# Two unused bf16 products per step in the first attention and in both memory attentions

## The chip, the cores and the metric

The kernel runs on one core of one Trainium2 chip. Its metric is the device time of one execution in microseconds (us); a time quoted for a kernel is the median of several runs. A core has five engines that run side by side: TensorE (PE, matrix products into PSUM banks; its weight loads are listed apart as PEld), VectorE (DVE), ScalarE (ACT), GpSimd (POOL) and SyncE (SP, which issues the weight transfers here). The profile also lists the clock granted to TensorE, as a share of full speed: 1.00 is 2.4 GHz and 0.50 is 1.2 GHz.

## The reference, cut to what matters

The program is a chain of blocks on 512 tokens of width 1024. The first block is a mixer with two banded attentions, a gated convolutional feed-forward, a state-space layer and a second feed-forward; the second block is a convolution layer, a memory attention, a gated feed-forward, a differential attention, a second memory attention and a last feed-forward. The change touches the place where two functions are computed:

```python
def band_attention(q, k, v, n_prev, bias, sinks):      # called twice in the first layer
    ...
        sc = jnp.einsum("bqkgd,bskd->bkgqs", qb, kb).astype(jnp.float32) * scale + bias
    ...
            p = jax.nn.softmax(sc, axis=-1)
    ...
        return jnp.einsum("bkgqs,bskd->bqkgd", p.astype(vb.dtype), vb)

def memory_cross_attention(h, mem, w_q, w_k, w_v, w_o):  # called twice in the second block
    ...
    s = jnp.einsum('bshd,bmhd->bhsm', q, k, preferred_element_type=jnp.float32) * MEM_HEAD_DIM ** -0.5
    p = jax.nn.softmax(s, axis=-1)
    o = jnp.einsum('bhsm,bmhd->bshd', p.astype(v.dtype), v).reshape(B, S, D_MODEL)
    return o @ w_o
```

The first layer has 8 heads of width 64 whose band covers the whole causal past, with a learned relative bias, and 8 heads of width 64 with a short window, a linear bias and a sink per head. The memory attention has 4 heads of width 256 over 256 memory tokens.

## The kernel before, in words

Each engine has its own instruction stream, written out by hand, and the streams meet at semaphores. There is no scheduler and no planner: the order on an engine is the order of the Python code.

The large matrix products are in `gemm` (L546): a weight slab arrives by DMA, ACT rounds it to an upper half (`w_hi`, L1791), POOL subtracts to get the lower half (`w_lo`, L504), and PE runs three products per 128x128 weight block (L564, L565, L566), 512 columns each, into one of four banks.

The attentions of the first layer and of the memory are all in `attention` (L592). A *unit* is one head and one tile of 128 queries, and one *step* m of the loop at L647 handles four units at once, each at another stage:

- `score(m)` (L613) computes the scores of unit m. In the first layer these are fp32 products of 64 rows (`qk`) of 128 to 512 columns. For units 0 to 31 an fp32 product of 128 rows adds the learned bias (`rel,flip`) over all columns, and a bf16 product adds the mask (`masks_b,ident_b`, 128 columns). For units 32 to 63 one bf16 product adds the linear bias (`alibi_b,ident_b`). In the memory they are two fp32 products of 128 rows and 256 columns. The score of unit m waits until ACT has taken the exponential of unit m-3.
- DVE takes the row maximum (L1156) and the scale (L1158 or L1163), ACT the exponential (L1837), DVE the reciprocal and the division (L1172, L1175).
- `turn(m-3)` (L626) transposes the probabilities of unit m-3 on PE; ACT copies them out of the bank (L1849).
- `outputs(m-4)` (L640) multiplies them with the values. In the first layer the output of one product has 64 rows.

After 8 units (first layer) or 4 units (memory) the outputs of a group are complete, and ACT and DVE read them out (L1856, L1187). The first `outputs` of a later group waits until DVE is done with that (L635).

The first attention has 64 units and so 64 + 4 = 68 steps, each memory attention 16 units and 16 + 4 = 20 steps. The differential attention has a loop of its own and does not use this function, so `peers` is 1 in every call that is made.

`keep_clock(n)` (L576) issues n bf16 products of a 128x128 identity with 384 columns of the mask table, into columns 128 to 511 of bank 7, whose content nobody reads there. It is called with 8 ahead of the first attention (L685) and with 6 ahead of each memory attention (L708). Inside the step it stands behind `if peers == 2`, which no call fulfils.

Of the kernel before, what the change touches and what calls it, by code (L numbers as in the profile page):

```python
# [155 lines left out]
def build(nc, A, out, stages=ALL):  # L156
# [4 lines left out]
    with ExitStack() as ctx:  # L161
# [176 lines left out]
        def score_bank(n, peers):  # L338

            return bank[n % 3] if peers == 1 else bank[(0, 1, 2, 4)[n % 4]]  # L340

        def turned_bank(k, peers):

            return bank[3 + k % 2 if peers == 1 else 3]
# [196 lines left out]
        def _(pe):  # L541
# [34 lines left out]
            def keep_clock(n):  # L576


                for _ in range(n):
                    pe.matmul(NORM_BANK[:, P:4 * P], ident_b[:], masks_b[:], start=True, stop=True,  # L580
                              skip_group_check=True)
# [10 lines left out]
            def attention(units, groups, peers=1, out=None):  # L592


                U = len(units)
                u0, t0, g0 = au[0], at[0], ag[0]
                group_of = {first: g for g, (first, _, _) in enumerate(groups)}
                nch = len(groups[0][2])
                ends = {last: g for g, (_, last, _) in enumerate(groups)}

                def score(m):
                    tiles = range(peers * m, peers * (m + 1))

                    if tiles[-1] >= 2 + peers:
                        pe.wait_ge(a_exp, u0 + tiles[-1] - 1 - peers)
                    for k in range(len(units[tiles[0]].scores)):
                        for n in tiles:
                            u = units[n]
                            if u.rel is not None and n % NT == 0 and k == 1:
                                pe.wait_ge(rel_buf[u.rel % 4], 16 * (u.rel // 4 + 1))  # L610
                            l, r, c0, w = u.scores[k]
                            last = k == len(u.scores) - 1
                            mm = pe.matmul(score_bank(n, peers)[:, c0:c0 + w], l, r, start=(k == 0), stop=last,  # L613
                                           skip_group_check=True)
                            if last:
                                mm.then_inc(a_score, 1)

                def turn(m):
                    u = units[peers * (m + 1) - 1]
                    src = a_prob_t[:, peers * m % PROBS, :]  # L620
                    pe.wait_ge(a_prob, t0 + m + 1)

                    if m >= 3 - peers:
                        pe.wait_ge(a_pt, t0 + m - 2 + peers)
                    for kt in range(u.nk // P):
                        mm = pe.transpose(turned_bank(m, peers)[:, kt * P:(kt + 1) * P], src[:, kt * P:(kt + 1) * P],  # L626
                                          ident[:])
                    mm.then_inc(a_turn, 1)

                def outputs(m):  # L630
                    u = units[peers * (m + 1) - 1]
                    if peers * m in group_of:

                        held = group_of[peers * m] * nch + nch - 2
                        if held > 0:  # L635
                            pe.wait_ge(a_ol, g0 + held) if out is None else pe.wait_ge(o_raw, held)
                    pe.wait_ge(a_pt, t0 + m + 1)
                    nk = u.nk // P
                    for v, kt, ch, lo, hi, t in u.pv:
                        mm = pe.matmul(bank[5 + ch % 2][lo:hi, t * P:(t + 1) * P], v,  # L640
                                       a_pt_t[:, m % 2, kt * P:(kt + 1) * P], start=(kt == 0),
                                       stop=(kt == nk - 1), skip_group_check=True)
                    mm.then_inc(a_pv, 1)

                T = U // peers
                turn_lag, out_lag = (3, 4) if peers == 1 else (1, 2)
                for m in range(T + out_lag + (0 if out is None else 2)):  # L647
                    if m < T:
                        score(m)
                    if peers == 2:  # L650
                        keep_clock(2)
                    if out is not None and peers * m - 6 in ends:
                        out(ends[peers * m - 6])
                    if peers == 2 and 0 <= m - out_lag < T:
                        outputs(m - out_lag)
                    if 0 <= m - turn_lag < T:
                        turn(m - turn_lag)
                    if peers == 1 and 0 <= m - out_lag < T:
                        outputs(m - out_lag)
                au[0] += U  # L660
                at[0] += U // peers
                ag[0] += len(groups) * nch

            def attn():
                st = ST["attn_in"]

                def fin(c, j):
                    if isinstance(c, int) and c >= 13:
                        v_turn(v_tmp[:, c % 2, :], c - 13, BANKS + st.chunk0 + c + 1, S, bank[5 + c % 2])
                        return  # L670
                    pe.wait_ge(q_sq, c + 1)

                    if not isinstance(c, int) or c >= 2:
                        pe.wait_ge(q_root, c - 1)

                    pe.matmul(bank[5 + j % 2][:], head_ones[:], sq[:, j % 2, :], start=True, stop=True)\
                        .then_inc(q_sum, 1)

                def after(c, j):
                    first_sum(c, j)  # L680
                    if isinstance(c, int) and c == 0:
                        pe.wait_ge(cst_ready, 4)
                    lagged(fin, 17)(c, j)
                gemm(st, xh, xl, S, x_ready(KD * nrm[0]), after, peel=4, tail=6)
                keep_clock(8)  # L685
                pe.wait_ge(q_ready, 13)
                pe.wait_ge(flip_done, 2)
                pe.wait_ge(v_ready, 2 + 5)
                vt[0] = 5
                attention(*UNITS["attn"])  # L690
                gemm(ST["attn_out"], oh, ol, S, lambda k: pe.wait_ge(a_ol, k + 1))
# [14 lines left out]
            def mem(l):  # L706
                gemm(ST[f"mem_q{l}"], xh, xl, S, x_ready(KD * nrm[0]), first_sum, peel=4)
                keep_clock(6)  # L708
                pe.wait_ge(bank_free, BANKS + ST[f"mem_q{l}"].chunk0 + KD)
                pe.wait_ge(v_ready, 2 + vt[0])  # L710
                g0 = ag[0]
                attention(*UNITS["mem"])
                gemm(ST[f"mem_out{l}"], oh, ol, S, lambda k: pe.wait_ge(a_ol, g0 + k + 1))
# [1687 lines left out]
```

## Time and profile before

| | |
|---|---|
| median of 3 runs | 3370.28 us |
| the three runs | 3376.12, 3351.67, 3370.28 us |
| time of the profiled execution | 3372.42 us |
| its span, first to last instruction | 3370.6 us |
| mean granted TensorE clock | 0.960 |
| PE busy | 3145.2 us, 93% of the span |
| DVE, ACT, POOL busy | 47%, 38%, 38% |
| first attention, first score to first product of its output projection | 154.37 to 319.84 us |
| first memory attention, the same | 2045.72 to 2092.44 us |
| second memory attention, the same | 2894.32 to 2937.86 us |

The span is the time from the first to the last instruction on the core; the time of the execution is 1.8 us more. A busy share is the time in which the engine had an instruction under way. On PE, ends are modelled, so a PE that is always busy need not be at its peak: at half the clock the same work shows as more busy time. What a stage is bound by is read from what the engines wait for in that stage, and from the granted clock beside it.

### The profile page before, as it was taken

To read this page: it belongs to the slowest core of one execution; us is meant where nothing else is said; L and a number is where in the kernel's file an instruction comes from. 1 tells how busy PE (TensorE), PEld (TensorE's weight loads), DVE (VectorE), ACT (ScalarE), POOL (GpSimd) and SP (SyncE) were. 2 spreads that over 40 slices of the span, in tenths; PEclk is the share of its full clock that TensorE was granted. 3 is DMA by queue.
4 is the path that set the end of the run, shared out by engine and by line. 5 is a ranking of instruction groups with operands and counts; after the bars stand their busy time and mean duration, and the time that the engine had idled before them with its cause. 6 is when DMAs were issued, how large, how long until landed. Compare 5 with 4: busy or idle time off the path is not lost.

```text
span 3370.6 us, 40942 instructions
## 1 busy us (share of the span) xinstructions
PE 3145.2 (93%) x13890; PEld 2426.7 (72%) x13890; DVE 1576.5 (47%) x2266; ACT 1270.1 (38%) x1983; POOL 1274.5 (38%) x495
## 2 busy tenths in 40 slices
PE   7999999998998899999866698999999999899998
PEld 5655888886675578888743587888876787788886
DVE  6445555337616725551445843333237765332322
ACT  3244444333334534442312343434333343344432
POOL 3300444442341044444554641444442244144443
PEclk9996999999998899999988899999999999999999
DMA  3200222332220022223200221222331123122232
GB/s 133 78 16 13 94 93 93 97 102 75 79 84 1 1 94 94 93 94 100 94 31 25 75 94 43 90 94 93 99 101 55 63 94 94 44 94 93 93 100 88
DMA packets 73288, 260.48 MB, mean 77 GB/s; under 512 B 8528, under 2 KB 8792, under 8 KB 72928
## 3 DMA queue, kind: packets, MB, share of 16 engines
q1 hardware_dynamic: 68400, 249.07, 23.1%
q10 hardware_dynamic: 4784, 10.05, 0.8%
q8 instruction: 62, 1.02, 0.1%
q14 instruction: 42, 0.34, 0.0%
HBM read 256.97 MB, written 2.12 MB: 77 GB/s over the span
## 4 chain that ended last, share of the span: by engine, by line
PE 51%; issue 30%; POOL 13%; DVE 4%; ACT 2%; DMA 0%; ACTq 0%; POOLq 0%; DVEq 0%; SPq 0%
PE bank L564 12%; PE bank L566 12%; PE bank L565 12%; POOL w_lo L504 12%; PE bank L733 2%; PE bank L734 2%; PE bank L735 2%; PE bank L640 1%; PE bank L795 1%; POOL m_lo L517 1%; PE bank L1021 1%; PE bank L613 1%; PE bank L819 1%; PE bank L1024 1%; PE bank L909 0%
## 5 line engine op out<-in xcount | busy, mean ns | idle before, releaser
L504 POOL TENSOR_TENSOR w_lo<-w_raw,w_hi 128x1024 fp32r<-128x1024 f32 x475 | 1219.1, 2569 | 1948.8 <-ACT w_hi L1791 1948.7
L564 PE MATMUL bank<-xh,w_hi 128*128 128x512 f32 x2136 | 865.6, 405 | 94.8 <-POOL w_lo L504 63.2
L565 PE MATMUL bank<-xl,w_hi 128*128 128x512 f32 x2136 | 854.4, 400 | 0.0
L566 PE MATMUL bank<-xh,w_lo 128*128 128x512 f32 x2136 | 853.6, 400 | 0.0
L1791 ACT ACTIVATE w_hi<-w_raw 128x1024 fp32r<-128x1024 f32 x475 | 500.8, 1055 | 713.3 <-DMA w_raw<-w_glu_out 157.6
L564 PEld LDWEIGHTS bank<-xh,w_hi 128*128 128x128 f32 x2136 | 407.1, 191 | 212.3 <-POOL w_lo L504 71.1
L565 PEld LDWEIGHTS bank<-xl,w_hi 128*128 128x128 f32 x2136 | 407.1, 191 | 100.9 <-issue 4.1
L566 PEld LDWEIGHTS bank<-xh,w_lo 128*128 128x128 f32 x2136 | 407.1, 191 | 99.8
L1126 DVE TENSOR_TENSOR xt<-bank,xt 128x512 f32 x72 | 49.8, 692 | 501.5 <-PE bank L566 501.5
L566 PE MATMUL bank<-hh,w_lo 128*128 128x512 f32 x704 | 279.1, 396 | 0.0
L564 PE MATMUL bank<-hh,w_hi 128*128 128x512 f32 x704 | 279.1, 396 | 0.0
L565 PE MATMUL bank<-hl,w_hi 128*128 128x512 f32 x704 | 279.1, 396 | 0.0
L1707 DVE TENSOR_TENSOR f_u<-bank,rstd 128x512 f32<-128x512 f32 x88 | 60.8, 691 | 276.7 <-PE bank L566 276.7
L565 PEld LDWEIGHTS bank<-hl,w_hi 128*128 128x128 f32 x704 | 132.6, 188 | 32.3
L564 PEld LDWEIGHTS bank<-hh,w_hi 128*128 128x128 f32 x704 | 132.6, 188 | 32.3
L566 PEld LDWEIGHTS bank<-hh,w_lo 128*128 128x128 f32 x704 | 132.6, 188 | 32.3
L1710 DVE TENSOR_TENSOR f_h<-f_y,f_u 128x512 f32<-128x512 f32 x88 | 150.6, 1712 | 7.2 <-ACT f_y L2211 0.3
L2216 ACT ACTIVATE hh<-f_h 128x512 f32 x88 | 55.6, 632 | 260.6 <-DVE f_h L1710 260.6
L1100 DVE TENSOR_TENSOR acc<-acc,sq 128x512 f32<-128x512 f32 x88 | 103.1, 1172 | 70.2 <-ACT sq L1782 70.2
L564 PE MATMUL bank<-oh,w_hi 128*128 128x512 f32 x320 | 128.8, 403 | 0.2 <-issue 0.2
L566 PE MATMUL bank<-oh,w_lo 128*128 128x512 f32 x320 | 127.8, 399 | 0.0
L565 PE MATMUL bank<-ol,w_hi 128*128 128x512 f32 x320 | 127.7, 399 | 0.0
(302 smaller groups left out, 4278.8 us busy)
## 6 DMA issues: line engine op xcount, KB each, us to landing
w_raw<-w_ffn_in SPq DMA_DIRECT2D x88, 512.0 KB, 3.5
w_raw<-w_glu_in SPq DMA_DIRECT2D x88, 512.0 KB, 3.4
w_raw<-w_ffn_out SPq DMA_DIRECT2D x48, 512.0 KB, 3.5
w_raw<-w_glu_out SPq DMA_DIRECT2D x48, 512.0 KB, 3.5
w_raw<-w_ssm_in SPq DMA_DIRECT2D x41, 512.0 KB, 3.5
w_raw<-w_mem_kv SPq DMA_DIRECT2D x32, 512.0 KB, 3.5
w_raw<-w_pw SPq DMA_DIRECT2D x24, 512.0 KB, 3.4
w_raw<-w_diff_in SPq DMA_DIRECT2D x24, 512.0 KB, 3.5
```

The source lines that it names most:

```text
L504: pool.tensor_tensor(w_lo[:, slot, :], w_raw[:, slot, :], w_hi[:, slot, :].bitcast(F32), ALU.subtract).then_inc(w_split, 1)
L564: pe.matmul(b, wh, hi[:, k, 0:n], start=(k == 0), stop=False)
L565: pe.matmul(b, wh, lo[:, k, 0:n], start=False, stop=False)
L566: mm = pe.matmul(b, wl, hi[:, k, 0:n], start=False, stop=last)
L733: pe.matmul(b, wh, hi[:, k, 0:n], start=(k == 0), stop=False)
L734: pe.matmul(b, wh, lo[:, k, 0:n], start=False, stop=False)
L735: mm = pe.matmul(b, wl, hi[:, k, 0:n], start=False, stop=(k == KD - 1))
L1100: dve.tensor_tensor(acc[:], acc[:], sq[:, j % 2, :], ALU.add).then_inc(x_acc, 1)
L1707: dve.tensor_tensor(f_u[:], bu[:], rstd[:], ALU.mult).then_inc(bank_free, 1)
L1710: dve.tensor_tensor(f_h[:], f_y[:], f_u[:], ALU.mult).then_inc(f_prod, 1)
L1791: act.activation(w_hi[:, slot, :], w_raw[:, slot, :], ACT.Copy).then_inc(w_half, 1)
L2216: act.activation(row(hh, p), f_h[:], ACT.Copy)\
```

## The change

The condition in the step loop is dropped, so that two of the unused products are issued in every step of the first attention and of both memory attentions, between the scores and the transposes. Nothing else differs; a line is gone, so that lines after 650 have a number that is lower by one in the changed kernel.

```diff
@@ -647,8 +647,7 @@
                 for m in range(T + out_lag + (0 if out is None else 2)):
                     if m < T:
                         score(m)
-                    if peers == 2:
-                        keep_clock(2)
+                    keep_clock(2)
                     if out is not None and peers * m - 6 in ends:
                         out(ends[peers * m - 6])
                     if peers == 2 and 0 <= m - out_lag < T:
```

The order of the instructions shows where they stand. On PE, in the second half of the first attention (units with the linear bias; L613 scores, L626 transpose, L640 outputs, L580 the unused products):

```order
 L613 MATMUL bank<-alibi_b,ident_b 128x128
+L580 MATMUL bank<-masks_b,ident_b 128x384 x2
 L626 MATMUL bank<-ident,a_prob_t 128x128 x2
 L640 MATMUL bank<-a_pt_t,v_tok 64x128
 L613 MATMUL bank<-qk 128x256
 L613 MATMUL bank<-alibi_b,ident_b 128x256
+L580 MATMUL bank<-masks_b,ident_b 128x384 x2
 L626 MATMUL bank<-ident,a_prob_t 128x128 x2
 L640 MATMUL bank<-a_pt_t,v_tok 64x128 x2
```

Each step has one pair, behind its last score product and ahead of its transposes; there are 68 of these pairs in the first attention.

On PE, at the start of a memory attention (the scores of units 0 to 3, the first transpose, then unit 4):

```order
-L613 MATMUL bank<-m_k,m_q 128x256 x8
+L613 MATMUL bank<-m_k,m_q 128x256 x2
+L580 MATMUL bank<-masks_b,ident_b 128x384 x2
+L613 MATMUL bank<-m_k,m_q 128x256 x2
+L580 MATMUL bank<-masks_b,ident_b 128x384 x2
+L613 MATMUL bank<-m_k,m_q 128x256 x2
+L580 MATMUL bank<-masks_b,ident_b 128x384 x2
+L613 MATMUL bank<-m_k,m_q 128x256 x2
+L580 MATMUL bank<-masks_b,ident_b 128x384 x2
 L626 MATMUL bank<-ident,a_prob_t 128x128 x2
```

The eight score products that stood in a row have a pair behind every two of them; each memory attention gets 20 pairs. In all there are 108 pairs, 216 products. The streams of DVE, ACT, POOL and SP are the same as before.

## Rows read from the trace of the kernel before

**Rows 1.** The page, part 1 (busy time, share of the span, instructions).

```profile
PE 3145.2 (93%) x13890; PEld 2426.7 (72%) x13890; DVE 1576.5 (47%) x2266; ACT 1270.1 (38%) x1983; POOL 1274.5 (38%) x495
```

**Rows 2.** Stretches: length, busy time per engine, granted clock, DMA share, GB/s.

```profile
158.00:178.00 20.00, 20.00 (x46) 9.16 (x44) 6.25 (x25) 4.32 (x15) 0.00 (x0) 0.50 0.13 44
179.00:240.00 61.00, 61.00 (x304) 35.29 (x302) 28.25 (x99) 24.48 (x76) 0.00 (x0) 1.00 0.05 17
241.00:270.00 29.00, 25.40 (x145) 15.29 (x144) 21.83 (x95) 16.27 (x63) 0.00 (x0) 1.00 0.00 1
271.00:320.00 49.00, 48.98 (x157) 27.34 (x156) 24.24 (x107) 18.60 (x74) 0.00 (x0) 0.50 0.00 1
323.00:340.00 17.00, 17.00 (x74) 13.70 (x73) 5.33 (x8) 5.66 (x8) 5.78 (x3) 1.00 0.25 75
```

**Rows 3.** Timeline of PE, scores of units 32 and 48, and a group's first outputs.

```profile
242.26 0.49 PE L613 MATMUL bank<-qk 64*128 64x128 f32 x2
...
269.25 0.65 PE L640 MATMUL bank<-a_pt_t,v_tok 128*64 128x128 f32 x4 [1.13 <-ACT a_pt_t L1849]
...
271.85 0.58 PE L613 MATMUL bank<-qk 64*128 64x128 f32 x1
```

**Rows 4.** The same, tail of the first attention and its output projection's start.

```profile
314.32 0.69 PE L626 MATMUL bank<-ident,a_prob_t 128*128 128x128 f32 x2
...
319.84 0.80 PE L564 MATMUL bank<-oh,w_hi 128*128 128x512 f32 x1
320.43 0.63 PE L565 MATMUL bank<-ol,w_hi 128*128 128x512 f32 x1
...
321.71 0.48 PE L565 MATMUL bank<-ol,w_hi 128*128 128x512 f32 x1
```

**Rows 5.** Who waited for whom, 154 to 320 us: total us, times, longest.

```profile
DVE a_stat L1156 <- PE bank L613: 69.4, 53, 5.4
...
PE bank L640 <- ACT a_pt_t L1849: 3.2, 4, 1.3
```

**Rows 6.** Who waited for whom, first memory attention, 2040 to 2092 us.

```profile
DVE a_stat L1156 <- PE bank L613: 17.8, 13, 3.8
...
PE bank L640 <- DVE ol L1187: 8.7, 3, 3.2
```

**Rows 7.** Timeline from 154 us, and line L580 alone (ns: min/median/max).

```profile
153.75 0.65 PE L580 MATMUL bank<-masks_b,ident_b 128*128 128x384 bf16 x3
...
L580 PE MATMUL bank<-masks_b,ident_b x20: 326/326/336, 152.9 to 2894.1; 128*128 128x384 bf16 x20
```

**Rows 8.** Timeline of PE ahead of the first attention (start, us, instruction, count).

```profile
152.94 1.46 PE L580 MATMUL bank<-masks_b,ident_b 128*128 128x384 bf16 x8
154.37 0.46 PE L613 MATMUL bank<-qk 64*128 64x128 f32 x2
157.18 0.49 PE L613 MATMUL bank<-rel,flip 128*128 128x128 f32 x2 [2.35 <-DMA rel<-rel_table]
```

**Rows 9.** DVE's row maximum (L1156), one per unit, in 154:181 and in 181:241 us.

```profile
L1156 DVE TENSOR_REDUCE a_stat<-bank x7: 291/425/693, 157.8 to 177.3; 128x1 f32<-128x128 f32 x2, 128x1 f32<-128x256 f32 x2, 128x1 f32<-128x384 f32 x2, 128x1 f32<-128x512 f32 x1
...
L1156 DVE TENSOR_REDUCE a_stat<-bank x24: 291/490/692, 181.4 to 237.8; 128x1 f32<-128x512 f32 x6, 128x1 f32<-128x128 f32 x6, 128x1 f32<-128x256 f32 x6, 128x1 f32<-128x384 f32 x6
```

**Rows 10.** Stretches of the two memory attentions, columns as in rows 2.

```profile
2062.70:2066.10 3.40, 3.40 (x12) 2.94 (x13) 0.00 (x0) 0.00 (x0) 0.00 (x0) 0.50 0.00 0
...
2912.80:2916.00 3.20, 3.20 (x14) 2.86 (x13) 1.00 (x4) 0.84 (x3) 0.00 (x0) 0.50 0.02 5
```

**Rows 11.** Timeline of PE: both memory attentions' first scores and first projection product.

```profile
2045.72 3.72 PE L613 MATMUL bank<-m_k,m_q 128*128 128x256 f32 x16
...
2092.44 0.48 PE L564 MATMUL bank<-oh,w_hi 128*128 128x512 f32 x1
...
2894.32 3.72 PE L613 MATMUL bank<-m_k,m_q 128*128 128x256 f32 x16
...
2937.86 0.48 PE L564 MATMUL bank<-oh,w_hi 128*128 128x512 f32 x1
```

## The prediction, made before the changed kernel ran

> **What bounds the kernel now.** I read the busy shares first: PE is busy for 93% of the span [rows 1], so anything added to PE has to be looked at for its cover. The 40 slices show that its granted clock is below full in a few places, one of them the first attention. So the second view is a table of stretches through it [rows 2]. The reader is to see two low stretches: from 158 to 178 us and from 271 to 320 us the clock is 0.50 (1.2 GHz), between and after them 1.00 (2.4 GHz). In the long one PE is busy for 48.98 of 49.00 us, and with 157 matmul records in 49 us it gets through less than with 145 in 29 us at full clock. Being busy does not bring the clock back there. What PE did before it fell at 271 us: it had stood idle for 1.13 us at the start of a group of outputs, and before that its steps were half-filled products of 64 rows or 64 columns [rows 3]. What it did when the clock rose again: the output projection had begun, 128x128x512 products without a gap [rows 4]; the clock was back two microseconds later, and stayed [rows 2].
>
> The third view is who waits for whom. In the first attention DVE's row maximum waits for PE's scores 53 times, 69.4 us in all, while PE waits four times for ACT's copy, 3.2 us in all [rows 5]. So PE sets the pace there at either clock, and a product that is added to it is paid for unless it falls into one of those four gaps. The memory attentions are alike: DVE waits 17.8 us for scores, and PE stands idle three times, 8.7 us in all, until DVE has read out a group of outputs [rows 6].
>
> **The price of a pair.** Three of the same products end 0.65 us after the first has started and the last one takes 0.326 us, so they start 0.162 us apart at full clock, and a pair costs 0.324 us [rows 7]. The upper bound is the eight in a row ahead of the attention: 1.43 us from the first to the next score, 0.179 each with both edges, 0.36 a pair [rows 8]. At half the clock I take 0.65 (the projection's products start 0.43 us apart at 0.50, three of them from 320.43 to 321.71 us [rows 4], and 0.23 apart at 1.00, 74 in 17 us [rows 2], so nearly twice). There are 68 + 20 + 20 = 108 pairs, 35 us at full clock without any cover. The Trainium skill (TensorE: Matmul & The Clock Gate, Back-to-back issue gap) says that in a stream of weight loads and matmuls even 512 columns take about 131 ns each; by that a pair of 384 columns would be at most 0.26 us and the 108 pairs at most 28 us, 7 us less. The row of 0.162 us disagrees with it for this very product, and the sum goes by the row.
>
> **The sum, against the profiled execution's 3372.4 us** (2.1 us above the median of the three).
>
> 1. Units 0 to 31, the ones with the learned bias: 32 pairs at 0.324, PE without a gap [rows 2] and 24 units in 60 us [rows 9]: +10.4 us.
> 2. The low stretch of 20 us at their start. It begins after PE stood idle for 2.35 us until the first bias table had landed [rows 8]; the pair of step 0 comes behind that wait and cannot prevent it. How soon the clock returns with denser steps no row shows. One end: the clock returns after the same seven steps, whose pairs then cost 0.65, +2.3 us. The other: it returns at once, and half of 20 us is saved, -10. I take -4, that it returns some 8 us earlier, since the projection brought it back in two microseconds and the added products are as full as those, but they are only a fifth of a low step (seven steps in 20 us [rows 9]).
> 3. Units 32 to 47, at full clock now, 29.6 us from the score of unit 32 to that of unit 48 [rows 3]: 16 pairs are 5.2 us, of which the four gaps [rows 5] take in one each, 1.3 us: +3.9 us, so 33.5 us.
> 4. Units 48 to 63, the same work at half clock, take 42.5 us (271.85 to 314.32) [rows 3, 4]. If the pairs keep the clock, they take the same 33.5 us: -9.0 us.
> 5. The four last steps, without scores, and the first products of the projection: 5.5 us at half clock (314.32 to 319.84) become 2.8 and four pairs, 1.3: -1.4. Four product starts at 0.43 instead of 0.23 us apart: -0.8. Together -2.2 us.
> 6. Memory attentions: 20 pairs each. In steps 4, 8, 12 and 16 the outputs wait anyway (for ACT's first copy and for the three groups), and the pair ahead of them lies in that wait, since what ends it (DVE's reading, behind ACT's exponential of a unit whose score stands ahead of the pair) does not depend on the pair. The other 16 cost 5.2 us each time: +10.4 us for both.
> 7. Behind three of these waits in the first memory attention, and behind one in the second, the clock falls for 3.4 us [rows 10]. The first takes 46.7 us, the second 43.5 [rows 11], so that a low stretch costs 1.6 us. A pair shortens the idle time ahead from 3.2 to 2.8 us; one end is that all four go, -6.4, the other that one more comes, +1.6. I take one less: -1.6 us.
>
> The sum is 10.4 - 4.0 + 3.9 - 9.0 - 2.2 + 10.4 - 1.6 = +7.9 us: **3380 us**. Nothing is added on another engine or queue, the bank's columns are read by nobody at that time, and the products signal no semaphore, so the only thing queued behind a pair is PE's own next transposes and, through them, the next score; DVE's row maximum will wait for PE longer and ACT's copies come later by as much. What pays is the two attentions' steps, what is gained is the clock.
>
> **Rivals.**
>
> A. *The clock is not kept.* Where PE is busy already, the pairs add nothing to its busy time, and it sits at 0.50 while it is busy for 48.98 of 49.00 us [rows 2]. The Trainium skill (TensorE: Matmul & The Clock Gate, The HAM clock gate) says that the gate goes by how busy the engine has recently been; by that rule pairs in a gapless stretch would change nothing about the clock, and only their price would be left. Against it: with the same busy share the units with the learned bias, which have full 128-row products, run at 1.00 for 61 us [rows 2], so what fills the busy time matters, and the pairs are of the full kind. The time: units 48 to 63 stay at 42.5 and pay 16 x 0.65, 52.9 us instead of 33.5, +19.4; the tail 5.5 + 2.6 instead of 4.1, and 0.8 for the projection, +4.8; the first stretch at its upper end, +6.3; the memory +1.6. With +7.9 that is +40 us, **3412 us**, slower. It decides at the group boundary near 270 us: if PE's clock falls there although a pair has gone into the gap, this rival holds. Chance 0.13.
>
> B. *Both cures work.* The first low stretch goes at once (-6.0 beyond step 2's value) and all four in the memory too (-4.8): -3 us, **3370 us**, no change. For it: the projection needed only two microseconds. Against it: the idle times of 2.35 and 2.8 us stay. Chance 0.20.
>
> C. *The clock falls late or for a part* in units 32 to 63, half of A's 19.4 us: **3390 us**. Chance 0.12.
>
> D. *The pairs are hidden*, since DVE's and ACT's chain takes over at once; then only steps 2, 4, 5 and 7 are left, with the pairs of step 4 free as well: -4.0 - 12.9 - 3.5 - 1.6 = -22, **3350 us**. The 69.4 us that DVE waits for PE [rows 5] speak against it. Chance 0.05.
>
> That the low stretch from 271 us is an accident of the profiled run is possible: the fastest of the three runs is 20.7 us below it, and without that stretch it would be 12.9 + 3.5 = 16 us shorter. This makes no difference to the changed kernel's time, only to what it is compared with.
>
> **The numbers.** The forecast has 0.47, A 0.13, B 0.20, C 0.12, D 0.05, and 0.03 are for what I don't see. The predicted time is that of the likeliest case. Its own bounds: steps 2 and 7 at their good ends give 3370, and the median may differ from a profiled run by some 10 us, as the three runs do; at their bad ends, with 0.36 us a pair (+3.9), 3394, and with case C's half 3403. The range of 3360 to 3403 leaves out A and most of D, 0.18. About 1% (34 us) is what a measurement of this kernel can tell from no change. Faster by over 1% would be below 3337, which no case reaches: 0.02. Slower by over 1% is above 3404: A and a part of the rest, 0.14. Within 1%: 0.84.
>
> **What the profile would show.** L580 grows from 20 to 236 products of 0.326 us at full clock. Step 1: units 8 to 31 at a pace of 2.8 instead of 2.5 us a unit, clock 1.00. Step 2: the first low stretch ends before 178 us. Steps 3 to 5: clock 1.00 from there into the projection, 33 to 34 us for each 16 units with the linear bias, and the attention as a whole, 165.5 us before, within 3 us of that. Steps 6 and 7: about 52 and 49 us for the two memory attentions, 1.6 less for each low stretch that goes, idle times of 2.8 us at three group boundaries. The prediction is wrong if the clock is 0.50 anywhere in units 32 to 63, if a pair costs clearly more than 0.36 us in a step, or if the first attention changes by more than 15 us either way.

## The result, and the profile after

The changed kernel took **3379.9 us** (median of 11 runs, 3377.5 to 3389.4), beside 3361.3 us for the kernel before (11 runs, 3349.9 to 3376.1). The ratio is 1.0053, with a 95% interval of 1.0033 to 1.0073: half a per cent slower, within the 1% of "no change". The number forecast, 3380, was met; what it is compared with was not 3370, since two of the three runs known then are among the four longest of those eleven. Its scatter of 26 us against the 12 of the changed kernel is part of the story. One run of all those below (3559.6 us, of `e7_one`, at a mean granted clock of 0.829) was a slow one, and the ratios are taken without it.

The profiled execution of the change took 3383.0 us, its span 3381.2. First the page's busy times, then the stretches that answer to [rows 2] (length, busy us and instructions per engine, granted clock, DMA share, GB/s):

```profile
PE 3156.5 (93%) x14106; PEld 2439.1 (72%) x14106; DVE 1579.9 (47%) x2266; ACT 1269.9 (38%) x1983; POOL 1273.7 (38%) x495
```

```profile
158.00:168.00 10.00, 10.00 (x21) 3.73 (x20) 2.52 (x10) 1.69 (x6) 0.00 (x0) 0.50 0.08 33
...
172.00:240.00 68.00, 68.00 (x353) 40.39 (x351) 28.05 (x102) 23.96 (x76) 0.00 (x0) 1.00 0.07 20
...
245.00:316.00 71.00, 68.59 (x391) 41.28 (x389) 47.16 (x206) 36.36 (x141) 0.00 (x0) 1.00 0.00 1
...
316.00:340.00 24.00, 24.00 (x104) 19.31 (x103) 8.26 (x12) 8.66 (x12) 9.26 (x4) 1.00 0.21 68
```

The long low stretch is gone: 1.00 from 172 us into the projection. The low stretch at the start is still there, 13.7 us long instead of 20.5. The timeline of PE through the first attention (start, us, instruction, count, idle time before it) answers to [rows 3, 4, 8]:

```profile
157.63 0.80 PE L613 MATMUL bank<-rel,flip 128*128 128x128 f32 x2 [3.35 <-DMA rel<-rel_table]
...
249.61 0.48 PE L613 MATMUL bank<-qk 64*128 64x128 f32 x2
...
263.31 0.65 PE L640 MATMUL bank<-a_pt_t,v_tok 128*64 128x128 f32 x4 [0.54 <-ACT a_pt_t L1848]
...
269.19 0.70 PE L613 MATMUL bank<-qk 64*128 64x256 f32 x2
269.82 0.28 PE L613 MATMUL bank<-alibi_b,ident_b 128*128 128x256 bf16 x1
269.94 0.49 PE L580 MATMUL bank<-masks_b,ident_b 128*128 128x384 bf16 x2
...
271.16 0.70 PE L613 MATMUL bank<-qk 64*128 64x256 f32 x2
...
278.46 0.65 PE L640 MATMUL bank<-a_pt_t,v_tok 128*64 128x128 f32 x4 [0.54 <-ACT a_pt_t L1848]
...
280.90 0.48 PE L613 MATMUL bank<-qk 64*128 64x128 f32 x2
...
311.21 0.50 PE L580 MATMUL bank<-masks_b,ident_b 128*128 128x384 bf16 x2
...
316.00 0.51 PE L564 MATMUL bank<-oh,w_hi 128*128 128x512 f32 x1
```

Unit 32 begins at 249.61, unit 48 at 280.90, the first step without a score at 311.21, the projection at 316.00. A full step in between takes 1.97 us (269.19 to 271.16), with the pair behind its bias product. The idle time at a group boundary is 0.54 us where it was 1.13. Its place is ahead of the third outputs of a group (unit 42 here, as at 269.25 us in [rows 3], which calls them the first). What these outputs wait for is DVE's readout of the group before and what follows from it: the row maximum of unit 45, its exponential, and ACT's copy for unit 42:

```profile
275.89 0.69 DVE L1186 TENSOR_TENSOR ol<-bank,oh 128x512 fp32r<-128x512 f32 x1 [0.81 <-ACT oh L1855]
276.50 0.41 DVE L1155 TENSOR_REDUCE a_stat<-bank 128x1 f32<-128x256 f32 x1
...
277.59 0.45 ACT L1836 ACTIVATE a_prob_t<-bank,a_stat 128x256 f32<-128x256 f32 x1
...
278.04 0.37 ACT L1848 ACTIVATE a_pt_t<-bank 128x256 f32<-128x256 f32 x1
```

The memory attentions, as [rows 11] (first scores, outputs that wait for a readout, first product of the projection):

```profile
2042.96 1.13 PE L613 MATMUL bank<-m_k,m_q 128*128 128x256 f32 x4
...
2061.66 2.08 PE L640 MATMUL bank<-a_pt_t,m_v 128*128 128x128 f32 x8 [2.84 <-DVE ol L1186]
...
2094.59 0.48 PE L564 MATMUL bank<-oh,w_hi 128*128 128x512 f32 x1
...
2896.91 1.13 PE L613 MATMUL bank<-m_k,m_q 128*128 128x256 f32 x4
...
2915.60 2.08 PE L640 MATMUL bank<-a_pt_t,m_v 128*128 128x128 f32 x8 [2.84 <-DVE ol L1186]
...
2930.86 1.16 PE L640 MATMUL bank<-a_pt_t,m_v 128*128 128x128 f32 x8 [2.84 <-DVE ol L1186]
...
2943.43 1.16 PE L640 MATMUL bank<-a_pt_t,m_v 128*128 128x128 f32 x8 [2.29 <-DVE ol L1186]
...
2948.43 0.47 PE L564 MATMUL bank<-oh,w_hi 128*128 128x512 f32 x1
```

They take 51.6 and 51.5 us, where they took 46.7 and 43.5. The outputs at 2061.66 need 2.08 us for eight products (1.16 at full clock): the clock is low behind the wait. In the second memory attention it is low behind the first wait and again from 2932 us, behind the second, but not behind the third:

```profile
2915.00:2921.00 6.00, 5.40 (x20) 4.59 (x21) 1.55 (x5) 0.84 (x3) 0.00 (x0) 0.50 0.00 0
2932.00:2935.00 3.00, 3.00 (x12) 2.20 (x11) 1.00 (x4) 0.65 (x3) 0.00 (x0) 0.50 0.02 5
2936.00:2948.00 12.00, 9.71 (x74) 8.55 (x74) 3.81 (x12) 3.81 (x11) 0.00 (x0) 1.00 0.00 1
```

From rows like these, one table for all profiled runs. "Low" is the time at clock 0.50 in the first attention; the memory columns have the number of low stretches behind them, each of 3.4 us but for one of 6.8 us in the change. "Between" is from the first attention's projection to the first memory attention.

| profiled run | units 0-31 | 32-63 and tail | first attention | low | between | memory 1 | memory 2 |
|---|---|---|---|---|---|---|---|
| before | 87.9 | 77.6 | 165.5 | 72 | 1725.9 | 46.7 (3) | 43.5 (1) |
| after | 95.8 | 66.4 | 162.2 | 14 | 1727.0 | 51.6 (3) | 51.5 (2, one of 6.8 us) |
| e1_attn_only | 95.8 | 66.4 | 162.3 | 14 | 1727.0 | 43.6 (1) | 45.0 (2) |
| e2_mem_only | 89.3 | 70.5 | 159.8 | 51 | 1721.7 | 51.6 (3) | 51.3 (3) |
| e3_late | 89.2 | 66.4 | 155.6 | 24 | 1724.1 | 46.7 (3) | 43.5 (1) |
| e4_gaps | 79.5 | 62.0 | 141.5 | 0 | 1724.7 | 42.0 (0) | 41.9 (0) |
| e5_before_again | 85.1 | 85.0 | 170.2 | 85 | 1721.8 | 43.6 (1) | 45.1 (2) |
| e6_rows | 86.3 | 72.2 | 158.5 | 14 | 1725.8 | 46.7 (3) | 43.5 (1) |
| e7_one | 85.8 | 63.3 | 149.1 | 14 | 1725.3 | 45.1 (2) | 43.5 (1) |
| e9_start_mem | 85.7 | 85.6 | 171.3 | 89 | 1725.7 | 42.0 (0) | 41.9 (0) |
| e10, e13 | 85.7, 86.2 | 63.6, 63.6 | 149.3, 149.8 | 14, 14 | 1722.9 twice | 43.6 (1) twice | 45.2, 45.1 (2) |
| e11_gaps_longer | 80.3 | 62.0 | 142.2 | 0 | 1723.9 | 42.1 (0) | 42.1 (0) |
| e12_mem_filled | 90.0 | 77.6 | 167.6 | 75 | 1724.1 | 46.9 (0) | 46.9 (0) |

### The profile page after: what moved, and what is told of

Read it like the earlier page. It is cut to its first block, busy times and chain, and to the rows that moved or that the text cites. A ratio compares the mean times of both kernels' runs of the same rounds, so it can differ in the third digit from the quotient of the medians.

```text
span 3381.2 us, 41374 instructions
## 1 busy us (share of the span) xinstructions
PE 3156.5 (93%) x14106; PEld 2439.1 (72%) x14106; DVE 1579.9 (47%) x2266; ACT 1269.9 (38%) x1983; POOL 1273.7 (38%) x495
## 4 chain that ended last, share of the span: by engine, by line
issue 49%; PE 27%; POOL 20%; DVE 3%; ACT 1%; POOLq 0%; ACTq 0%; DMA 0%; DVEq 0%; SPq 0%
POOL w_lo L504 19%; PE bank L564 7%; PE bank L565 7%; PE bank L566 7%; PE bank L1020 1%; PE bank L640 1%; PE bank L613 0%; PE bank L908 0%; PE bank L1023 0%; PE bank L675 0%; PE bank L1037 0%; PE bank L982 0%; DVE s_dk L1520 0%; PE bank L962 0%; DVE s_ea L1513 0%
```

## The experiments

The kernels differ from the kernel before by the lines shown; nch is 1 in the first attention and 2 in the memory.

**e1_attn_only**

```diff
-                    if peers == 2:
+                    if nch == 1:
                         keep_clock(2)
```

> Pairs in the 68 steps of the first attention only, none in the memory attentions. Theory T1 (the profiled run of before had a low-clock stretch of 50 us in the units with the linear bias that its typical run, 11 us shorter, has only in part; the two memory attentions of the change pay 5 us each whatever the run): the first attention as in the changed kernel, 162 us, clock 1.00 from 171 us on; time 3380 less 10 to 13 us, so 3367 to 3370, and its runs lie within some 10 us. Rival T2 (the first attention gains 3 us against every run of before, and the memory attentions or what comes behind them cost the other 22): 3358 us.

Measured: 3367.3 us (3363.7 to 3371.5), ratio to before 1.0002 (0.9986 to 1.0018), clock 1.00 from 171 us. T1's number, and T2's 3358 us is out. The 12.6 us to the changed kernel come with the memory pairs, as their own price and as low stretches; by the table 51.6 + 51.5 less 43.6 + 45.0, 14.5 us.

**e2_mem_only**

```diff
-                    if peers == 2:
+                    if nch == 2:
                         keep_clock(2)
```

> Pairs in the 20 steps of each memory attention only. T1: 5 us for each, 1.6 us more or less for each 3.4 us low stretch that comes or goes: 3361 + 10 = 3371 us, with the wide scatter of before (25 us), since the low stretch of the first attention is there in some runs. T2: 3361 + 22 = 3383 us.

Measured: 3383.5 us (3364.5 to 3393.4), ratio 1.0047 (1.0021 to 1.0074), that is 16 us more than before (21 by the medians) in place of T1's 10. T2's number came out, but not its reason: in the profile the first attention has a low stretch of its own again, beginning at 285 us, and the stretch between the attentions is 4 us *shorter* than before. T1 was mis-sized: there are six low stretches in the memory and not four, which makes 3 us more; the rest of the difference has no row, and the eight runs lie 29 us apart.

**e3_late**

```diff
-                    if peers == 2:
+                    if nch == 1 and m >= 32:
                         keep_clock(2)
```

> Pairs only in steps 32 to 67 of the first attention (the units with the linear bias and the tail); none in units 0 to 31, none in the memory. T1: the 32 pairs of units 0 to 31 are pure price (10.4 us) except that they end the first low stretch some 6 us earlier, worth 3; the late ones keep the clock at 1.00 from unit 32 into the projection. 3368 - 10 + 3 = 3361 at the least good, and as low as 3354 if the low stretch at the start is as in before; its scatter is small. T2: no different from e1 but for the 10 us: 3348 us.

Measured: 3356.5 us (3353.5 to 3362.2), ratio 0.9977 (0.9958 to 0.9996), faster than before by little, within T1's 3354 to 3361, and with a scatter of 9 us. Units 32 to 63 take the same 66.4 us as in the change; units 0 to 31 take 6.6 us less, although the start's low stretch is 24 us here and 14 in e1. Its length turned out to be chance: with bare units 0 to 31 it is 14 us in e5, e6, e7, e10 and e13, and 20 to 24 in before, e2, e3 and e12. With 14 us in both (e1 and e10), and without the wait for the first bias table (3.3 and 3.7 us), the 32 pairs cost 92.5 - 82.0 = 10.5 us. T2 gave 8 us too little.

**e4_gaps**: no pairs; 120 products stand where PE waits. In the linear-bias units they are ahead of the outputs of units 34, 42, 50 and 58, so at four places and not at the five steps that the expectation names.

```diff
+                            if u.rel is not None and n == 0 and k == 1:
+                                keep_clock(12)
                             if u.rel is not None and n % NT == 0 and k == 1:
                                 pe.wait_ge(rel_buf[u.rel % 4], 16 * (u.rel // 4 + 1))
...
                         if held > 0:
+                            if nch == 2:
+                                keep_clock(14)
                             pe.wait_ge(a_ol, g0 + held) if out is None else pe.wait_ge(o_raw, held)
+                    if nch == 1 and m >= 34 and m % 8 == 2:
+                        keep_clock(6)
                     pe.wait_ge(a_pt, t0 + m + 1)
```

> No pairs in the steps; the unused products stand only where TensorE would idle: 12 ahead of the first wait for the bias table (idle 2.4 to 3.4 us), 6 in steps 34, 42, 50, 58 and 66 ahead of the outputs that wait 1.1 to 1.3 us for ACT, 14 ahead of each of the three waits for a group's readout in each memory attention (idle 2.3 to 3.2 us). If the clock falls because of these idle times and not because of what the steps are filled with: clock 1.00 throughout the three attentions, nothing paid, 3350 (fastest run of before) less up to 10 for the first stretch and 6 for the memory: 3336 to 3345 us. If it falls because the steps of the linear-bias units are too thin, the long low stretch still comes in some runs, and the scatter stays: 3350 to 3360 us.

Measured: **3342.3 us** (3340.1 to 3352.5), ratio 0.9935 (0.9911 to 0.9958). PE's timeline ahead of the first bias table, at two group boundaries of the linear-bias units, and at a readout wait of the memory; then the stretch:

```profile
153.78 2.12 PE L580 MATMUL bank<-masks_b,ident_b 128*128 128x384 bf16 x12
156.50 0.49 PE L615 MATMUL bank<-rel,flip 128*128 128x128 f32 x2 [0.59 <-DMA rel<-rel_table]
...
244.06 1.14 PE L580 MATMUL bank<-masks_b,ident_b 128*128 128x384 bf16 x6
245.54 0.65 PE L646 MATMUL bank<-a_pt_t,v_tok 128*64 128x128 f32 x4 [0.35 <-ACT a_pt_t L1855]
...
258.64 1.14 PE L580 MATMUL bank<-masks_b,ident_b 128*128 128x384 bf16 x6
259.94 0.65 PE L646 MATMUL bank<-a_pt_t,v_tok 128*64 128x128 f32 x4 [0.15 <-ACT a_pt_t L1855]
...
2033.18 2.44 PE L580 MATMUL bank<-masks_b,ident_b 128*128 128x384 bf16 x14
2036.51 1.16 PE L646 MATMUL bank<-a_pt_t,m_v 128*128 128x128 f32 x8 [0.89 <-DVE ol L1193]
```

```profile
236.00:270.00 34.00, 31.47 (x175) 18.30 (x174) 25.54 (x116) 19.72 (x78) 0.00 (x0) 1.00 0.01 1
```

The idle times, 2.2 to 4.5 us ahead of the bias table in the profiles without filling, 1.1 to 1.3 and 2.3 to 3.2 us at the other places, have become 0.6, 0.2 to 0.4 and 0.9 or less, nothing begins later (259.94 - 245.54 = 14.4 us a group, as before at full clock), and the clock is 1.00 in all three attentions. The linear-bias steps are as thin as before, so thin steps can hold the clock once these idle times are filled. That the idle time itself makes the fall is not parted from another reading: the six products are also six full products more per group, and no run has just these six elsewhere in the group with the idle time left; e7_one comes nearest. One run took 3352.5 us at a mean clock of 0.969 (0.973 in the profiled one), so the clock was not kept everywhere in every run.

**e5_before_again**: the kernel before, unchanged.

> The kernel before, unchanged, profiled once more. T1: the long low-clock stretch in the units with the linear bias begins by chance at one of the group boundaries (at 271 us in the first profile; at 283 us in the run with pairs in the memory only, whose first attention is the same as before). So it begins elsewhere or not at all here, and the linear-bias part with its tail takes between 62 (none) and 78 us; the other parts of the execution agree with the first profile within 5 us. T2 (the scatter of before has another source): 78 us again.

Measured: 3371.2 us. The clock fell at 251.5 us, earlier than in the first profile, and the part took 85 us, not at most 78: a fall at the first boundary costs more than I had allowed. The stretch between the attentions is 4 us shorter than in the first profile. PE's timeline there:

```profile
249.42 0.38 PE L626 MATMUL bank<-ident,a_prob_t 128*128 128x128 f32 x2
251.12 0.82 PE L640 MATMUL bank<-a_pt_t,v_tok 128*64 128x128 f32 x4 [1.33 <-ACT a_pt_t L1849]
251.88 1.22 PE L613 MATMUL bank<-qk 64*128 64x256 f32 x2
```

The score product that follows takes 1.22 us instead of 0.70. The fall comes right behind the idle time of 1.33 us.

**e6_rows**: as e3, each product over 32 rows.

```diff
-                    if peers == 2:
-                        keep_clock(2)
+                    if nch == 1 and m >= 32:
+                        keep_rows(2)
...
+            def keep_rows(n):
+                for _ in range(n):
+                    pe.matmul(NORM_BANK[:, P:4 * P], ident_b[0:32, :], masks_b[0:32], start=True, stop=True,
+                              skip_group_check=True)
```

> As the run with pairs only in steps 32 to 67, but each of the two products has 32 rows instead of 128 (the same 384 columns, so the same time on TensorE, a quarter of the array). If the clock goes by busy time alone: no difference, linear-bias part 66.4 us, clock 1.00, 3356.5 us. If it goes by how much of the array works: the clock falls again in some of the linear-bias units, that part takes 70 to 85 us, and the time is 3365 to 3375 us with a wide scatter. (T1 in the prediction's words: full products are what keeps it.)

Measured: 3366.3 us (3360.2 to 3372.0), ratio 1.0003 (0.9984 to 1.0021). The time is what "how much of the array works" gave, for another reason: the clock stayed at 1.00 in the linear-bias units, as "busy time alone" had it, but a step is longer. Line L585 alone (ns: min/median/max), then PE's timeline of one step:

```profile
L585 PE MATMUL bank<-masks_b,ident_b x72: 321/326/332, 240.9 to 311.7; 32*128 32x384 bf16 x72
```

```profile
261.84 0.70 PE L618 MATMUL bank<-qk 64*128 64x256 f32 x2
262.47 0.28 PE L618 MATMUL bank<-alibi_b,ident_b 128*128 128x256 bf16 x1
262.69 0.49 PE L585 MATMUL bank<-masks_b,ident_b 32*128 32x384 bf16 x2
263.11 0.44 PE L631 MATMUL bank<-ident,a_prob_t 128*128 128x128 f32 x2
...
264.06 0.70 PE L618 MATMUL bank<-qk 64*128 64x256 f32 x2
```

The product has the same 0.326 us, but starts 0.22 us behind the start of the bias product, where the 128-row one starts 0.12 behind it (269.82 to 269.94 in the change), and the step is 2.22 us instead of 1.97. What in the 32 rows costs this is open. So the experiment does not settle whether fullness counts: these steps had no idle time left in which the clock could fall.

**e7_one**: as e3 with `keep_clock(1)`.

> One full product instead of two in steps 32 to 67 of the first attention, none elsewhere. If half the filling is enough: clock 1.00, linear-bias part about 64 us (62.0 without any and at full clock, 66.4 with two), 3354 us. If not: a low stretch comes in some runs, 3360 us and more.

Measured: 3355.7 us (nine runs, 3354.5 to 3364.5), ratio 0.9978 (0.9960 to 0.9996); the linear-bias part takes 63.3 us at clock 1.00. One product was enough in this profile, with idle times of 0.8 to 1.0 us left at the boundaries. Of the 3.1 us that it saves against two, the medians show 0.8.

**e9_start_mem**: e4 without the `keep_clock(6)`.

> The products in idle time as in the run before (3342 us), but without the 6 at the group boundaries of the linear-bias units: 12 ahead of the wait for the bias table and 14 ahead of each readout wait of the memory. If the idle time at those boundaries is what lets the clock fall: the long low stretch is back in some runs, linear-bias part 62 to 78 us, the time 3342 to 3358 with a median near 3352 and the scatter of before. If the start's low stretch was what mattered: 3342 us, small scatter.

Measured: 3356.7 us (3347.6 to 3371.6), ratio 0.9972 (0.9955 to 0.9989): the scatter of before, 24 us, is back, and its longest runs lie above the 3358 us that I had given as the upper end. In the profile the clock fell at the first unfilled boundary, at 251.5 us, which is within the idle time. PE's timeline, and the stretches around it:

```profile
251.70 1.11 PE L644 MATMUL bank<-a_pt_t,v_tok 128*64 128x128 f32 x4 [1.33 <-ACT a_pt_t L1853]
```

```profile
250.00:251.00 1.00, 0.37 (x3) 0.14 (x2) 0.86 (x6) 0.38 (x2) 0.00 (x0) 1.00 0.00 0
251.00:252.00 1.00, 0.30 (x2) 0.30 (x3) 0.93 (x5) 0.66 (x4) 0.00 (x0) 0.77 0.00 0
252.00:253.00 1.00, 1.00 (x5) 0.67 (x4) 0.53 (x3) 1.00 (x4) 0.00 (x0) 0.50 0.00 0
...
252.00:322.00 70.00, 69.98 (x220) 38.28 (x218) 36.22 (x159) 27.38 (x109) 0.00 (x0) 0.50 0.00 1
```

Six products at four places are what parts this from e4: 85.6 against 62.0 us. That is the difference of two single profiles; by the medians it is 14 us. In this profile the bias table landed 0.7 us later than in that of e4, 1.24 us of idle time were left behind the 12 products, and the clock was low from 159 to 173 us.

**e10_restore** and **e13_restore_again** (the same kernel): `if nch == 1 and m >= 56`.

> Pairs only from step 56 of the first attention on. In three of three profiles with that attention's steps bare the clock fell right behind an idle time of PE of 1.1 to 1.3 us at a group boundary (251, 271, 284 us) and stayed at 0.50 for the rest of the attention. Theory G: the fall is made by the idle time, and the thin steps cannot raise the clock again; what pairs do inside low steps is open. If they raise it (as the first low stretch suggests, 14 us with pairs and 20 to 24 without): the clock is 0.50 from some boundary to a few us behind step 56, then 1.00. If they only keep it: 0.50 to the end of the attention, and the last steps take 3.6 us (2.95 + 0.65) each. Time 3355 to 3375.

> The kernel with pairs only from step 56 on, once more, since the clock had not fallen before step 56 in its first profile. In five of six profiles with bare steps it fell at 251, 271 or 284 us. If it has fallen, and pairs raise it: 0.50 up to a few us behind step 56 and 1.00 from there, step 60 to 63 at 1.96 us each. If pairs only keep it: 0.50 to the end, 3.6 us a step, linear-bias part 80 us or more. Without a fall: 63.6 us again, and the question stays open.

Measured: 3352.4 and 3353.1 us; the clock did not fall ahead of step 56 in either. Whether pairs can raise it within thin steps stays open; the reason given for it in the first expectation, that they had shortened the start's low stretch, falls with these two runs, in which that stretch was 14 us without them. In each of them PE stood idle for 1.33, 1.13 and 1.13 us at three boundaries with bare steps, and the clock stayed at 1.00. Both show what a run without the long low stretch costs: about 3353 us.

**e11_gaps_longer**: e4 with 18 for 12 and `17 if m < 16 else 13` for 14. The condition counts units, and the last wait is ahead of unit 12, so that all three waits of a memory attention got 17.

> The run with the products in idle time only (3342 us), with more of them where it still left idle time: 18 instead of 12 ahead of the first bias table's wait (1.2 us were left in one profile, and the clock fell behind it), 17 instead of 14 at the first two readout waits of a memory attention (0.9 us left) and 13 at the last (none left). If the idle time is covered in every run: the first attention 140 to 142 us, both memory attentions 42 us, 3341 us with a scatter below 10 us. If 18 is too many when the table lands early, up to 0.5 us more.

Measured: **3339.6 us** (3338.7 to 3344.6), ratio 0.9916 (0.9889 to 0.9943). As expected, with a scatter of 6 us in six runs: the lowest median and the smallest scatter of all, though its ratio's interval overlaps that of e4.

**e12_mem_filled**: pairs with `if nch == 2`, and `keep_clock(12)` ahead of the readout waits.

> Pairs in all steps of both memory attentions, and 12 products more ahead of each of their three readout waits; the first attention as before. It parts the price of the memory pairs (steps, 5.2 us in the sum) from the low stretches, which came six times of six with pairs in the profiled runs. Each memory attention 42.0 (full clock, no pairs) + 5.2 = 47.2 us and clock 1.00; the pairs' own price is wrong if it is over 48. The first attention: 142 to 172 us, with a fall of the clock behind one of the group boundaries or none.

Measured: 3376.9 us; both memory attentions 46.9 us at clock 1.00:

```profile
2044.92:2091.84 46.92, 44.80 (x301) 36.85 (x301) 20.01 (x70) 16.69 (x54) 0.70 (x1) 1.00 0.04 12
2894.43:2941.35 46.92, 44.79 (x301) 36.85 (x301) 20.00 (x70) 16.69 (x54) 0.61 (x1) 1.00 0.03 12
```

The 20 pairs cost 4.9 us against the 42.0 of e4, and the other 4.6 to 4.7 us of the 51.5 and 51.6 in the change are the 10.2 us that each attention spends at half clock. The first attention took 167.6 us, with a fall at 272 us.

## Why the prediction was right, point by point

The number held by luck in part: the first attention came out 3.2 us below the sum and the memory 4.1 us above it. Profile against profile, the span grew by 10.6 us: -3.3 in the first attention (the sum has -0.1 without the projection), +12.9 in the memory (+8.8), the rest +1.0. The mechanism, pairs that are paid in the steps and a clock that is kept from unit 32 on, was right but for the low stretches, at the start (step 2) and in the memory (step 7).

- **Price of a pair.** Right: a full linear-bias step grew from 1.64 to 1.97 us and a full memory step from 1.98 to 2.30, so 0.32 to 0.33. L580 has 236 products with a median of 0.326 us.
- **Steps 1 and 2, units 0 to 31.** Forecast +6.4, measured +7.9. The pairs are 10.4 (10.5 by e1 and e10). The low stretch was 13.7 us in place of 20.5, worth 3.4, as I had it but not for my reason: it is as short in five runs without pairs there, and nothing shows that pairs shorten it. The bias table came 1.0 us later (3.35 against 2.35 us of waiting).
- **Step 3, units 32 to 47.** Mis-sized: +1.7 us for +3.9. I let each of four gaps take in one pair, 1.3 us. PE's idle time from unit 32 to unit 48 went from 3.6 to 1.1 us, so 2.5 us were hidden: the two gaps of 0.4 us in a group are gone, and the one at the boundary shrank from 1.13 to 0.54 us, by two pairs. In the rows of the readout above, nothing that these outputs wait for stands behind the pairs at 275.24 and 277.21 us: the score of unit 45 is ahead of both, and the transposes of unit 42, behind the second, end at 277.91 us, before ACT has done the exponential that stands ahead of its copy. The 29.6 us of before also had their last 1.1 us at half clock, some 0.6 us that the change does not pay; 0.4 us stay without a row.
- **Steps 4 and 5.** The clock was kept: -12.2 for -9.0 (the same mis-sizing). The tail takes 4.8 us and not 4.1, so -0.7 for -1.4; the start of the projection gains 0.9 where I had 0.8. The 33 to 34 us that I had for each 16 units with the linear bias were 31.3 and 30.3.
- **Step 6, the memory pairs.** 4.9 us each where I had 5.2 (e12). The readout waits do hide the pair ahead of them: at full clock the step with the wait takes 5.41 us from score to score with pairs (e12) and without (e4).
- **Step 7 failed.** I took three low stretches in place of four; there were five, one of them of 6.8 us, together 20.5 us of half clock for 13.7: +3.1 us for -1.6. A pair ahead of the wait shortens it from 3.17 to 2.84 us (the last of each attention from 2.3 or 2.4 to 2.3), and this was not enough in five of six waits, nor in six of six of e2. Without pairs the clock fell at 27 of 48 waits, 20 of the 32 of 3.17 us and 7 of the 16 shorter ones (the table's eight runs with neither pairs nor filling there). Why a slightly shorter wait should bring more falls is open: the pairs also change the time from one wait to the next, 13.9 instead of 13.0 us. Filling the wait to 0.9 us or less (e4, e9, e11, e12) was enough in all.

**The rivals.** A is out: no clock below 1.00 in units 32 to 63 of any profile with pairs there, nor in that of the single product. The pairs had no low stretch to end there, since the clock had not fallen when they began and the idle times were down to 0.54 us, so A's premise, that pairs cannot raise the clock in a gapless stretch, was not tried. Two of the change's eleven runs took 3387.7 and 3389.4 us at mean clocks of 0.966 and 0.964, where the other nine have 0.967 to 0.968; where their clock was low, no profile shows. The rows of e9, like [rows 2], show PE busy for 69.98 of 70.00 us at 0.50 without getting the clock back. The Trainium skill (TensorE: Matmul & The Clock Gate, The HAM clock gate) has the gate go by how busy the engine has been; by the busy time of the profile these rows disagree with that as the whole rule. B did not happen (the start's low stretch and the memory's were still there), nor C nor D. What I named an accident and set aside is the larger finding: the long stretch begins by chance at one of the group boundaries (251.5, 251.5, 271, 272 and 285 us in five profiles) or not ahead of step 56 (e10, e13), so that the kernel before takes from 3350 to 3376 us. Against its typical run the change gains less in the first attention than against the profiled one, and the 13 us of the memory are paid in full.

## What to carry to other kernels

Unused products that keep TensorE's clock belong into its idle times, where they cost nothing here, and not into every step of a loop in which it sets the pace: about 38 us separate the same idea done with 216 products in the steps (1.0053) and with 120 in the waits (0.9935). Look for the wait right ahead of the fall, fill all but a fraction of a microsecond of it, and leave the steps alone. And when a kernel scatters by 0.8%, profile it more than once before taking a profile's loss for the typical one.

## What the runs showed that I had not expected

- The clock fell from 1.00 to 0.50 at an idle time of 1.33 us in e5 and e9, and behind it PE stayed there for 70 us while it was busy for 69.98. What decides it is open: seven profiles have 15 idle times of 1.1 to 1.3 us between bare steps at full clock, and five brought the fall and ten did not.
- Products of 32 rows between products of 128 rows cost a step 0.25 us more than full ones, though each is listed with the same 0.326 us.
- Most of the scatter between runs goes with the clock: 26 us before, 12 with the pairs, 6 in e11. In 25 runs of the kernel before, the time and the mean granted clock have a correlation of -0.99 (3350.7 us at 0.969, 3382.6 at 0.956).
